# Opening stage of a decoder step in another order: input rows first, low-rank projection next, memory keys and values last

## The reference

```python
def rms_norm(x, g, eps=NORM_EPS):
    y = xf * lax.rsqrt(jnp.mean(xf * xf, axis=-1, keepdims=True) + eps)
    return (y * g.astype(jnp.float32)).astype(x.dtype)

def mem_kv(mem, g, w_kv, k_g):
    k, v = jnp.split(rms_norm(mem, g) @ w_kv, [W_MEM], axis=-1)
    return (rms_norm(k.reshape(bsz, m, MEM_HEADS, MEM_HD), k_g),
            v.reshape(bsz, m, MEM_HEADS, MEM_HD))

# in a_layer
    xn = rms_norm(h, norm_g)
    proj = jnp.concatenate([prev_xn[:, None, :].astype(xn.dtype), xn], axis=1) @ w_in
    cur = proj[:, 1:, :n_sh]
    mixed = cur + (proj[:, :-1, :n_sh] - cur) * mu
    log_w = -jax.nn.softplus(-(w0 + jnp.tanh(wd) @ w_up).astype(f32)) - 0.5
    a = jax.nn.sigmoid((a0 + ad @ a_up).astype(f32))
```

## Time and profile before

| | |
|---|---|
| median of 3 runs | 2493.67 us (2489.96 to 2497.48) |
| profiled execution | 2497.91 us, its span 2496.3 us |
| TensorE busy | 2199.6 us, 88% of the span |
| VectorE, ScalarE, GpSimd busy | 892.4, 622.9, 317.9 us |
| mean granted TensorE clock | 0.938 of full speed |
| first TensorE instruction of `front` | 12.79 us |
| first TensorE instruction of `rwkv_pairs` | 77.77 us |

### The profile page before, as it was taken

How to read it: one execution, slowest core, us unless ns; L and a number is a source line. 1 busy time by engine, 2 the same in 40 slices (tenths; PEclk the granted TensorE clock), 3 DMA queues, 4 the chain that set the end, 5 groups by cost and what they waited for, 6 DMA issues and landing times. The chain is left out here.

```text
span 2496.3 us, 47130 instructions
## 1 busy us (share of the span) xinstructions
PE 2199.6 (88%) x20794; PEld 1437.5 (58%) x20794; DVE 892.4 (36%) x1735; ACT 622.9 (25%) x1393; POOL 317.9 (13%) x289
## 2 busy tenths in 40 slices
PE   7999999999999999967994999969977788699399
PEld 4586675856758567546442555535656556577243
DVE  3252453624436344232002303240023577344500
ACT  6222223222232222222003112120023466222200
POOL 0000110201102011010001022001100366122000
PEclk9999999999999999976997999989987799899599
DMA  6000000000000000050201112001120000698211
GB/s 239 28 19 19 27 17 13 29 27 27 20 10 29 27 28 12 23 209 1 106 34 55 40 65 104 1 0 42 34 76 1 1 1 1 213 318 282 121 52 38
DMA packets 50847, 148.96 MB, mean 60 GB/s; under 512 B 11427, under 2 KB 20963, under 8 KB 49236
## 3 DMA queue, kind: packets, MB, share of 16 engines
q1 hardware_dynamic: 39284, 100.07, 11.4%
q0 software_dynamic: 11360, 45.88, 5.1%
HBM read 124.14 MB, written 21.79 MB: 58 GB/s over the span
## 5 line engine op out<-in xcount | busy, mean ns | idle before, releaser
L819 PE MATMUL psum<-xT,rw_w 128*128 128x384 f32 (+1 forms) x1152 | 420.0, 493 | 2.8 <-PEq L169 2.8
L1813 PE MATMUL psum<-kvq_w,xT 128*128 128x384 f32 (+1 forms) x864 | 282.6, 489 | 12.8 <-POOL kvq_w L1767 12.8
L819 PEld LDWEIGHTS psum<-xT,rw_w 128*128 128x128 f32 x1152 | 200.3, 190 | 107.4 <-issue 11.2
L1813 PEld LDWEIGHTS psum<-kvq_w,xT 128*128 128x128 f32 (+1 forms) x864 | 158.9, 185 | 134.8 <-issue 22.2
L302 PE MATMUL psum<-xT,gq_w 128*128 128x292 f32 (+2 forms) x480 | 149.5, 475 | 9.8 <-POOL gq_w L1413 9.8
L302 PEld LDWEIGHTS psum<-xT,gq_w 128*128 128x128 f32 x480 | 92.9, 194 | 66.0 <-issue 38.4
L1350 DVE COPY rwkv_sa_sb<-psum 128x64 f32<-128x64 f32 x96 | 21.6, 225 | 264.8 <-PE psum L1027 264.8
L1718 PE MATMUL psum<-xT,yT 128*128 128x512 f32 (+1 forms) x216 | 98.4, 606 | 13.6 <-DMA xT<-in_w_out 13.6
L1161 ACT COPY rwkv_r_sb<-psum 128x64 f32<-128x64 f32 x96 | 20.4, 213 | 339.7 <-PE psum L1012 307.5
L786 POOL DMA_DIRECT2D out<-rwkv_s x6 | 5.7, 944 | 774.2 <-ACT rwkv_out_p L1182 774.2
L1718 PE MATMUL psum<-xT,y_r 128*128 128x512 f32 (+1 forms) x216 | 98.0, 604 | 1.4 <-PEq L169 1.4
(11 more groups left out here) (413 smaller groups left out, 3800.1 us busy)
## 6 DMA issues: line engine op xcount, KB each, us to landing
xT<-in_cache_k SPq DMA_DIRECT2D x64, 384.0 KB, 6.3
samp_vp<-in_cache_v POOLq DMA_DIRECT2D x64, 384.0 KB, 5.0
rw_w<-in_w_in SPq DMA_DIRECT2D x28, 512.0 KB, 3.8
kvq_w<-in_kv_w SPq DMA_DIRECT2D x4, 1536.0 KB, 6.4
gq_w<-in_b_in SPq DMA_DIRECT2D x10, 512.0 KB, 3.7
front_w<-in_mem_w_kv SPq DMA_DIRECT2D x2, 2048.0 KB, 14.6
x_rows<-in_x_p SPq DMA_DIRECT2D x8, 512.0 KB, 14.4
xT<-in_w_out SPq DMA_DIRECT2D x8, 512.0 KB, 10.8
```

Of the source, the lines that this page charges most:

```text
L819: mm = pe.matmul(out, w[:, load % 2, k, :], xT[:, k, a:b], start=(k == 0), stop=(k == KC - 1))
L1813: mm = pe.matmul(bank[0:r, j % 6, 0:W], xT[:, k, n * P:n * P + r], w[:, i % 2, k, :], start=(k == 0), stop=(k == KC - 1))
```

## The change

Nothing is computed otherwise; the same operations stand in another order on each engine, and the memory is turned in PSUM banks 4 to 7 instead of 0 to 3. `keys_values`, `turns`, `squares`, `normed`, `out`, `key_squares`, `key_roots`, `keys_out`, `sums` and `keys` are as before.

```diff
         @block.sync
             sp.dma_start(base[:, :], i["const0"]).then_inc(base_loaded, 16)
-            for n in range(2):
-                sp.dma_start(mx[:, n, :], mem[n * P:(n + 1) * P, :]).then_inc(mx_loaded[n], 16)
             sp.dma_start(vecs[:, :], i["vecs"]).then_inc(vecs_loaded, 16)
-            sp.dma_start(w[:, 0, :, :].rearrange("p k c -> p (k c)"), i["mem_w_kv"][0]).then_inc(w_loaded[0], 16)
             for n in range(NT):
...
             sp.dma_start(x_sb[NS:last, NT, :], i["shift"]).then_inc(x_loaded[NT], 16)
-            sp.dma_start(w[:, 1, :, :].rearrange("p k c -> p (k c)"), i["mem_w_kv"][1]).then_inc(w_loaded[1], 16)
+            sp.dma_start(lw[:, :, :].rearrange("p k c -> p (k c)"), i["w_in"][18]).then_inc(lw_loaded, 16)
+            for n in range(2):
+                sp.dma_start(mx[:, n, :], mem[n * P:(n + 1) * P, :]).then_inc(mx_loaded[n], 16)
+            for layer in range(2):
+                sp.dma_start(w[:, layer, :, :].rearrange("p k c -> p (k c)"), i["mem_w_kv"][layer]).then_inc(w_loaded[layer], 16)
...
         @block.tensor
             pe.wait_ge(base_loaded, 16)
+            turns(GROUPED[0])
+            turns(GROUPED[1])
+            pe.wait_ge(act_out, NTILE)
+            pe.wait_ge(dve_out, NTILE)
             for j in range(4):
...
-                    mm = pe.transpose(bank[:, j, k * P:(k + 1) * P], mx[:, n, kk * P:(kk + 1) * P], ident[:, :])
+                    mm = pe.transpose(bank[:, 4 + j, k * P:(k + 1) * P], mx[:, n, kk * P:(kk + 1) * P], ident[:, :])
                 mm.then_inc(mem_turned, 1)
-            keys_values(0)
-            turns(GROUPED[0])
-            keys_values(1)
-            turns(GROUPED[1])
-            turn_keys(0)
             pe.wait_ge(lw_loaded, 16)
-            pe.wait_ge(act_out, NTILE)
-            pe.wait_ge(dve_out, NTILE)
             for a, b in COLS:
...
+            keys_values(0)
+            keys_values(1)
+            turn_keys(0)
             turn_keys(1)
         @block.scalar
             act.wait_ge(cleared, 1)
+            squares(GROUPED[0])
+            squares(GROUPED[1])
             for n in range(2):
                 act.wait_ge(mx_loaded[n], 16)
                 link(nc.scalar.activation(sq[:, n, :], mx[:, n, :], ACT.Square, accum_out=mss[:, n:n + 1]))
             inverse_root(mrstd[:, :], mss[:, :], D, mrstd_ready)
+            for n in range(NTILE):
+                out(n)
...
+            key_squares(0)
+            key_roots(0)
+            key_squares(1)
+            keys_out(0)
+            key_roots(1)
+            keys_out(1)
         @block.vector
...
             for n in GROUPED[0]:
                 dve.wait_ge(x_loaded[n], 16)
                 normed(n)
-            sums(0)
+                if n >= 1:
+                    out(n - 1)
             dve.wait_ge(rstd_ready, 2)
...
             for n in GROUPED[1]:
-                out(n)
-            keys(1)
+                dve.wait_ge(x_loaded[n], 16 if n < NT else 32)
+                normed(n)
+                out(n - 1)
+            dve.wait_ge(mrstd_ready, 1)
+            for n in range(2):
+                nc.vector.tensor_scalar(mx[:, n, :], mx[:, n, :], mrstd[:, n:n + 1], None, ALU.mult).then_inc(mxh_ready, 1)
+            out(NTILE - 1)
...
+            dve.wait_ge(kgain_loaded, 16)
+            sums(0)
+            keys(0)
+            sums(1)
+            keys(1)
```

More of the change, by code:

```diff
@@ L359, in _ @@
             sp.dma_start(x_sb[NS:last, NT, :], i["shift"]).then_inc(x_loaded[NT], 16)
-            sp.dma_start(w[:, 1, :, :].rearrange("p k c -> p (k c)"), i["mem_w_kv"][1]).then_inc(w_loaded[1], 16)
+            sp.dma_start(lw[:, :, :].rearrange("p k c -> p (k c)"), i["w_in"][18]).then_inc(lw_loaded, 16)
[3 more added lines that the diff above has]
+                sp.dma_start(w[:, layer, :, :].rearrange("p k c -> p (k c)"), i["mem_w_kv"][layer]).then_inc(w_loaded[layer], 16)
             a, width = _ROW["memk0"]
             sp.dma_start(kgain[:, :], i["rows2"][a:a + 2 * width].partition_broadcast(P)).then_inc(kgain_loaded, 16)
-            sp.dma_start(lw[:, :, :].rearrange("p k c -> p (k c)"), i["w_in"][18]).then_inc(lw_loaded, 16)
             for n, c in enumerate((6, 0)):
@@ L489, in _ @@
                 nc.scalar.copy(mxT[:, 4 * half:4 * half + 4, n * P:(n + 1) * P],
[L490 to L494, removed]
-                out(n)
[L496 to L501, removed]
+                               bank[:, 4 + j, :].rearrange("p (k t) -> p k t", k=4)).then_inc(mxT_ready, 1)
             for j, (a, b) in enumerate(COLS):
@@ L515, in _ @@
                     nc.scalar.activation(lora[0:HS, c:d], lora[0:HS, c:d], ACT.Tanh)
-            keys_out(1)
             act.wait_ge(mixed, 3)
@@ L565, in _ @@
             link(nc.vector.tensor_scalar(omu[:, :], vec(vecs, "mu"), -1.0, 1.0, ALU.mult, ALU.add))
[L566 to L571, removed]
             dve.wait_ge(g_loaded, 16)
@@ L576, in _ @@
                 normed(n)
-            sums(0)
+                if n >= 1:
+                    out(n - 1)
             dve.wait_ge(rstd_ready, 2)
[L579 to L586, removed]
-            for n in GROUPED[1]:
-                out(n)
-            keys(1)
+            for n in GROUPED[1]:
+                dve.wait_ge(x_loaded[n], 16 if n < NT else 32)
[5 more added lines that the diff above has]
+            out(NTILE - 1)
+            dve.wait_ge(mxT_ready, 4)
+            nc.vector.tensor_tensor(mxg[:, :, :], mxT[:, :, :], bcast(vec(vecs, "memg0").unsqueeze(2), [P, KC, MEMT]),
+                                    ALU.mult).then_inc(mxg0_ready, 1)
             for j, (a, b) in enumerate(COLS):
```

## The result

The changed kernel takes 2511.99 us (median of 4 runs, 2508.83 to 2512.40) against 2493.05: ratio 1.0072, 95% interval 1.0054 to 1.0089: slower by 0.7%. The forecast was 2514.5, in a range of 2508 to 2522. The profiled execution was the fastest of the four, 2508.83, span 2507.2, and that of the kernel before (2497.91) was slower than all four of its timed runs (the slowest is 2497.48), so the two spans lie only 10.9 apart.

A forecast was written before the change was run, and what follows sets the result against it. TensorE's queue, busy 88% of the span, was taken as the bound. Next stage 97.1 against 77.8 gives 19.3, plus 1.5 for the clock, so 21 us slower: 2514.5 us, range 2508 to 2522.

The forecast's parts named there:

- 5, last copy of an input tile starts: Input turning: VectorE's scaling and copying, 1.79 us a tile, set the pace; memory's scaling precedes the last copy, at 42.8.
- The bounds named for the range: First root -0.8 to +1.1, tile 2's rate -0.9, clock -1.5 to +2, runs 3 either side; A reaches 2522.
- Step 1: Input's first root on ScalarE: five squares paced by the loads, then the root, done at 16.2 us, bounds 15.4 to 17.3.
- step 6: TensorE without a break: memory turned, low-rank product, two memory products, until 88.0; layer 0's keys and both gains hidden.
- The ring (step 4): Turning tile 2 needs ScalarE's copy of tile 0, queued behind three roots until 30.0; TensorE idle some 9 us.
- the tail (step 7): Layer 1's keys behind the last product, formerly beside the low-rank product: 8.1 us, then barrier 1.0, next stage at 97.1.
- the lost cover: ScalarE's input squares and two roots, 16.7 us, nearly all beside layer 0's product before, have nothing beside them.
- Step 8: TensorE's clock low after the 9 us gap, 0.5 us more; low rate in the low-rank product, 1 us mean.
- Rival A: TensorE's clock falls, or never rises, during the half-busy turning: 25 us slower in all, 2519; chance 0.18.
- Rival B: ScalarE's copies don't wait for the memory's root, so TensorE is 9 us earlier: +10 to +12, 2505; chance 0.05.
- Rival C: Not slower: the program from 1000 us on meets low-clock stretches otherwise and gives back the 21 us; chance 0.03.
- signs of being wrong: Tile 2 turned before ScalarE's third root; second stage before 94 or after 103; its start-to-end time differing by over 8 us.

The follow-up runs named there:

- the two series: The changed kernel measured twice, unedited the second time: median 2511.99 us (ratio 1.0072) in the first series, 2518.06 us (ratio 1.0094) in the second.
- the first two experiments: Copies first and Products covered, each one edit to the changed kernel: 2508.94 us and 2511.58 us.
- their sum: Changed kernel with both edits, ScalarE's copies ahead of the memory's root and two thirds of the low-rank product behind the memory products: 2504.66 us, ratio 1.0045.
- Copies first: Changed kernel with ScalarE copying turned input tiles as soon as turned, the memory's squares and root behind some of these copies: 2508.94 us, ratio 1.0061.
- Cover removed: Kernel before the change with only the two memory products, and the steps that go with them, moved behind the input's turning: 2508.33 us, ratio 1.0059.
- Products covered: Changed kernel with the low-rank product's second and third part moved behind the two memory products: 2511.58 us.
- Idle time filled: Changed kernel with seven products that nothing reads put into TensorE's idle time at the stage's end: 2514.41 us, ratio 1.0086.
- Old loads: Changed kernel with SyncE's queue of loads in the order from before the change: 2527.43 us, ratio 1.0125.

## Why the prediction was right

Point by point, forecast and measured:

| step | forecast | changed kernel |
|---|---|---|
| 1, first root done | 16.2 | 17.1 |
| 2, second root | 24.0 | 24.8 |
| 3, memory's root | 29.4 | 30.15 |
| 4, tile 2 turned from | 30.0 | 30.77 |
| 5, last copy of an input tile starts | 42.8 | 43.66 |
| 6, low-rank product starts | 45.2 | 45.97 |
| 6, end of layer 1's product | 88.0 | 88.3 |
| 7, next stage | 97.1 | 97.26 |
| 8, clock, next stage's first 48 matmuls against 16.67 | +0.5 | +1.4, then -0.3 |

The mechanism is the one that was forecast: the release of tile 2, the waits and the tail stand in the trace where the steps put them. The time is less sharp a success: 2514.5 lies between the medians of the two series, 2.5 above the one and 3.6 below the other. The bounds named for the range also add up to 2508.3 and 2520.6, not to 2508.5 and 2519.5; the range of 2508 to 2522 holds both.

Step 1 was 0.9 short: the first tile landed 0.5 later than counted, the second square waited 0.99 for its tile, and from there the squares started 1.27 apart, where ScalarE alone takes 1.17, so the loads, as forecast, set their pace, but later. This ran through to step 6, where the last tile's copy is shorter than a full one's. The ring (step 4) and the tail (step 7) are shown by the first two experiments and their sum; the lost cover by the third. The claim of step 6 that the keys of layer 0 and both gains hide holds: the three large products follow each other with no gap. The error shrinks to 0.3 there because the sum added full durations, 42.8 us from the low-rank product to the end of layer 1's, and the records overlap by 0.2 each (measured 42.4).

Of the 19.5 us, then: the ring costs 5.1; the tail some 5.4; the other 9.0 are the lost cover, less what the new load order gives back. The idle times in the two traces place these 9.0: TensorE's first wait (with the gap that stood before layer 0's product) is 2.9 longer, the part of the ring wait that **Copies first** leaves is 3.0, and the waits for VectorE's pairs and for the last copy are 2.9 longer, 8.8 in all. In the runs that priced these two, the cover was worth 14.3 with the old loads (a ring wait of 3.21 within it) and the new loads 7.3, a difference of 7.0. Of the 2 us between 7.0 and 9.0, 1.61 may be the wait for the last copy ahead of the memory's turning, which the kernel of **Cover removed** doesn't have; no run tests that.

Step 8 had the right mean (+0.5) for a wrong reason, which is luck. I tied the low clock after the stage to the length of the gap, and took 9 us for it; of the 8.9 us behind the last product TensorE is idle for 7.0, in two parts. With such a tail the first 48 matmuls took 18.03, 16.35, 16.55 and 17.08 us; after gaps of 2.8 us they took 16.67, 18.03, 16.67 and 14.97. The length made no difference that these show; only gaps of 1 us gave 14.97 both times. The 1 us that I took for the low-rank product didn't come either in the two executions of the changed kernel (14.90, with the memory turned in 1.94); in **Products covered**, **Idle time filled** and **Old loads** the low clock cost 2.8, 1.7 and 2.6 us at that place.

Rival A was no other outcome but a part of some executions: where nothing had been edited up to that point, the memory's turning took 1.94 twice and 3.65 and 3.47 once each; in the kernels with edits ahead of it, it took 1.94, 2.92 and 3.65. Whether such executions make up the 6 us between the changed kernel's two medians isn't shown: the profile of the slower series has none of it. The Trainium skill's rule (TensorE: Matmul & The Clock Gate, "Part 1: The HAM clock gate"), that activity releases the throttle, agrees with the trace where TensorE was busy without a break (in **Products covered** the granted clock was 0.50 from 46 to 49 us, in the low-rank product's first part, and 1.00 from 52 on, and layer 0's product always ran at the full rate behind the low-rank one). Which of the two this turning brings, no run here settles. Rival B fell with the order on ScalarE: the copy of tile 0 starts at 30.06, with the end of the third root. Its price was too high as well, 9 us against the 5.1 of **Copies first**. Rival C fell too: from the next stage to the end, taken as the median less the start in the profiled execution, before has 2415.3 (2417.1 in the second series), after 2414.7, the experiments 2415.5 to 2420.2 and the second series 2420.8. No kernel is shorter there by more than that spread, and what makes it I haven't found.

One of my own signs of being wrong did show. I had named a time from the next stage's start to the end that differs from before by over 8 us, and in the first profile it differs by 8.6 (2409.9 against 2418.5). The second profile of the same kernel has 2420.2, and over all ten profiles this time runs from 2409.9 to 2425.2, so the sign was narrower than what single executions differ by.

## What to carry to other kernels

When work is reordered on an engine that is full, look for what ran beside it on the others: the product moved to the end here took no longer itself (13.90 us, 16.37 before), but nine squares and two roots lost their cover, and its own epilogue came to lie bare at the barrier. Read the order on each engine against the ring of buffers: two roots ahead of a small copy stopped TensorE for 8.7 us and VectorE for 8.3, and moving the later root away brought TensorE back 5.1 us sooner. And keep something long that doesn't depend on the last product for behind it.

## What the runs showed of the hardware

The granted clock of the same instructions differed between executions. In four of them, with the same order up to that point and TensorE busy for 1.09 us in every 1.79 of the turning, the memory's turning behind it ran at the full rate twice (granted 1.00 from 44.2 to 46.0 us in the changed kernel) and at the low one twice (0.50 from 44.5 to 48.0 in **Products covered**), at a cost of up to 2.8 us in the stage.

A gap of 2.8 us was enough for a low stretch behind it in three executions of four, and 7 us of idle time cost the first 48 matmuls of the next stage no more (up to 18.03 us after either). In the changed kernel the granted clock is already 0.50 ahead of the next stage (from 94 to 97 us), in the kernel before only from 79.0 on, 1.2 us after that stage began.

Filling idle time with products that nothing reads went with the full rate (layer 0's product 13.97 instead of 16.37, the next stage's first run 14.97 instead of 16.67). In the old order the whole kernel was 2.7 us faster, just clear of no difference; in the changed kernel no time was gained.

The record of the granted clock is not to be trusted at the start of the kernel before: it reads 1.00 from 19 to 24 us, where a 512-column record of layer 0's product takes up to 1.19 us, against 0.59 later. The low rate there is therefore read from durations.
